# The last matrix product of a transformer block, cut into seven half-size products

## The chip, the core and the metric

The kernel runs on one core of a Trainium2 chip. The number compared is the device time of one execution, in microseconds (us), from the start of the program to its end. The core has a matrix engine (TensorE, PE in the profile, with its weight loads as PEld), a vector engine (VectorE, DVE), a scalar engine (ScalarE, ACT), a general engine (GpSimd, POOL) and a sync engine (SP), which here only issues DMA transfers. Each works through a queue of its own, in order, and waits on semaphores that the others raise.

## The reference, cut to what matters

Two transformer blocks are computed for 512 tokens of width 1024, with float32 inputs and output. The change is in the last line of the second block, a gated feed-forward layer with 2816 hidden features:

```python
FFN_HIDDEN = -(-(8 * D_MODEL) // (3 * 256)) * 256          # 2816 = 22 * 128
h = rms_norm(x, norm_ffn[l])
x = x + (jax.nn.silu(h @ w_gate[l]) * (h @ w_up[l])) @ w_down[l]
return x
```

The down projection multiplies a [512 x 2816] matrix, called A here, by `w_down`, [2816 x 1024], called B, and adds the product to x, which is the output.

## The kernel before, in words

**Three terms.** Each operand is split in two, both written in the type fp32r: the high part is a copy of the operand, the low part is the operand minus its high part. A product is three matmuls into the same bank of PSUM: high by high, low by high, high by low.

**Chunks.** The weights come in chunks of 128 rows by 512 columns, and all chunks of the kernel are in one list, `CH`. A slot of 8 KB per partition holds up to four chunks and is filled by one DMA; three slots (0, 1 and 2) take turns in the feed-forward layer. SyncE issues the DMAs in the order of the list, each when the slot's former chunks are used up (`slot_free`). For each chunk ScalarE writes the high part to one of eight places in `CHH` (so at most eight chunks can be ahead of TensorE: chunk c waits until c-8 is done), and VectorE then subtracts and writes the low part over the raw chunk (`low`). Both do this in `split_chunks`, called with the chunk number that is to be reached; `ahead(c, 5)` is five chunks beyond the one that TensorE is planned to use.

**Gate and up.** For four features at a time (of 128 hidden features each; 22 in all, the last turn has two) `fg` computes h @ w_gate, ScalarE applies silu, and `fu` computes h @ w_up. At the end of each `fu` VectorE multiplies the two (`up_evac`), ScalarE makes the high part of the product in `AFH`, and VectorE its low part in `AFL`. That gives A, transposed: feature by token.

**Down.** `seg("wd0")` and `seg("wd1")` compute the left and the right 512 columns of the output. Each goes over 22 chunks; for each chunk over four row blocks of 128 tokens, with three matmuls each: 2 x 22 x 4 x 3 = 528 matmuls of 512 columns. At the end of each half VectorE adds four banks to x in memory (`out_x`), and SyncE stores the result. GpSimd has nothing to do in this stage. The order of the work is written out by hand; there is no scheduler.

## Time and profile before

| | |
|---|---|
| median of three runs | 1574.17 us (1571.76 to 1575.76) |
| span of the profiled execution | 1570.6 us, from the first to the last instruction |
| TensorE busy | 1536.9 us, 98% |
| VectorE, ScalarE, GpSimd busy | 64%, 53%, 13% |
| first matmul of the down projection | begins at 1447.51 us |
| last matmul of the down projection | begins at 1566.96 us |

The profiled execution is one run of the same program; its span leaves out what lies before the first and behind the last instruction, so it is some 3.6 us below the median. TensorE's matmuls are pipelined: a row's duration (0.39 us) is longer than the step from one matmul to the next (0.23 us), and the step is what counts for time. For the other engines, instructions that are issued back to back also overlap a little, so that a group of several is shorter than its count times the duration of one.

### The profile page before, as it was taken

To read this page: it belongs to the slowest core of one execution; us is meant where nothing else is said; L and a number is where in the kernel's file an instruction comes from. 1 tells how busy PE (TensorE), PEld (TensorE's weight loads), DVE (VectorE), ACT (ScalarE), POOL (GpSimd) and SP (SyncE) were. 2 spreads that over 40 slices of the span, in tenths; PEclk is the share of its full clock that TensorE was granted. 3 is DMA by queue.
4 is the path that set the end of the run, shared out by engine and by line. 5 is a ranking of instruction groups with operands and counts; after the bars stand their busy time and mean duration, and the time that the engine had idled before them with its cause. 6 is when DMAs were issued, how large, how long until landed. Compare 5 with 4: busy or idle time off the path is not lost.

```text
span 1570.6 us, 20022 instructions
## 1 busy us (share of the span) xinstructions
PE 1536.9 (98%) x7872; PEld 1247.3 (79%) x7872; DVE 1007.2 (64%) x1681; ACT 832.5 (53%) x1459; POOL 210.5 (13%) x278
## 2 busy tenths in 40 slices
PE   9999999999999999999989999999999999999999
PEld 8877777788877888888877766888778888888887
DVE  4267977865479998999787786575765333434231
ACT  5278776554456888888863434435434333333220
POOL 1000014522234000000062101111201000000000
PEclk9999999999999999999999999999999999999999
DMA  6122121114547999999943111031212323223232
GB/s 233 65 81 79 56 71 65 54 54 150 214 161 231 375 421 421 421 422 421 326 149 107 54 54 54 28 108 54 81 58 78 108 81 108 92 82 121 67 112 90
DMA packets 78641, 235.89 MB, mean 150 GB/s; under 512 B 6960, under 2 KB 9424, under 8 KB 66256
## 3 DMA queue, kind: packets, MB, share of 16 engines
q1 hardware_dynamic: 68288, 207.62, 36.3%
q10 hardware_dynamic: 6624, 14.88, 2.5%
q0 software_dynamic: 3632, 12.08, 2.0%
q8 instruction: 63, 1.03, 0.3%
q14 instruction: 34, 0.28, 0.1%
HBM read 221.97 MB, written 12.60 MB: 149 GB/s over the span
## 4 chain that ended last, share of the span: by engine, by line
PE 84%; DVE 11%; ACT 2%; issue 1%; DMA 1%; POOL 0%; SPq 0%; DVEq 0%; ACTq 0%; POOLq 0%
PE bank L109 80%; PE bank L112 4%; DVE low L134 2%; DVE REST L124 1%; DVE REST L134 1%; DVE REST L137 1%; ACT REST L115 1%; DVE AL L124 1%; DVE REST L146 1%; DVE REST L143 1%; DVE REST L130 1%; ACT REST L118 1%; ACT CHH L118 0%; DVE R L124 0%; DVE st L140 0%
## 5 line engine op out<-in xcount | busy, mean ns | idle before, releaser
L124 DVE TENSOR_TENSOR low<-slot,CHH 128x1024 fp32r<-128x1024 f32 (+1 forms) x300 | 298.0, 1037 | 117.5 <-ACT CHH L118 116.5
L118 ACT ACTIVATE CHH<-slot 128x1024 fp32r<-128x1024 f32 (+1 forms) x300 | 258.8, 900 | 128.7 <-PE bank L109 56.6
L134 DVE SCALAR_TENSOR_TENSOR low<-slot,smalls,CHH 128x512 fp32r<-128x512 f32 (+1 forms) x232 | 170.3, 766 | 191.2 <-ACT CHH L118 187.3
L109 PE MATMUL bank<-AH,CHH 128*128 128x512 f32 (+1 forms) x640 | 248.5, 388 | 0.2 <-DVE AL L124 0.2
L109 PE MATMUL bank<-AL,CHH 128*128 128x512 f32 (+1 forms) x640 | 242.8, 379 | 0.0
L109 PE MATMUL bank<-AH,low 128*128 128x512 f32 (+1 forms) x640 | 242.6, 379 | 0.0
L118 ACT ACTIVATE CHH<-slot,smalls 128x512 fp32r<-128x512 f32 (+1 forms) x232 | 154.6, 701 | 137.8 <-PE bank L109 68.2
L109 PE MATMUL bank<-CHH,AH 128*128 128x512 f32 x512 | 215.2, 420 | 3.8 <-DVE low L134 2.8
L109 PE MATMUL bank<-low,AH 128*128 128x512 f32 x512 | 200.8, 392 | 0.0
L109 PE MATMUL bank<-CHH,AL 128*128 128x512 f32 x512 | 200.2, 391 | 0.0
L109 PE MATMUL bank<-CHH,XTF 128*128 128x512 f32 x512 | 161.2, 396 | 1.9 <-DVE REST L121 1.1
L109 PEld LDWEIGHTS bank<-AH,CHH 128*128 128x128 f32 x640 | 120.4, 188 | 23.3 <-issue 1.2
L109 PEld LDWEIGHTS bank<-AL,CHH 128*128 128x128 f32 x640 | 120.4, 188 | 23.1
L109 PEld LDWEIGHTS bank<-AH,low 128*128 128x128 f32 x640 | 120.6, 188 | 20.6
L115 ACT ACTIVATE REST<-REST 128x512 f32<-128x512 f32 (+4 forms) x193 | 98.0, 518 | 46.1 <-POOL REST L124 19.2
L109 PEld LDWEIGHTS bank<-CHH,AH 128*128 128x128 f32 x512 | 96.9, 189 | 29.6 <-issue 6.9
L109 PEld LDWEIGHTS bank<-low,AH 128*128 128x128 f32 x512 | 96.1, 188 | 21.3
L109 PEld LDWEIGHTS bank<-CHH,XTF 128*128 128x128 f32 x512 | 93.6, 188 | 24.0 <-DVE low L124 4.9
L109 PEld LDWEIGHTS bank<-CHH,AL 128*128 128x128 f32 x512 | 96.7, 189 | 14.9
L109 PE MATMUL bank<-low,XTF 128*128 128x512 f32 x256 | 99.9, 390 | 0.0
L118 ACT ACTIVATE REST<-bank 128x512 f32<-128x512 f32 (+6 forms) x166 | 62.5, 400 | 70.3 <-PE bank L112 40.7
L109 PE MATMUL bank<-REST 128*128 128x128 f32 (+8 forms) x688 | 90.0, 306 | 4.9 <-ACT REST L115 2.7
(191 smaller groups left out, 2395.4 us busy)
## 6 DMA issues: line engine op xcount, KB each, us to landing
slot<-in_w_in SPq DMA_DIRECT2D x35, 1024.0 KB, 5.1
slot<-in_w_exp_gate SPq DMA_DIRECT2D x32, 1024.0 KB, 13.0
slot<-in_w_exp_up SPq DMA_DIRECT2D x32, 1024.0 KB, 13.2
slot<-in_w_exp_down SPq DMA_DIRECT2D x32, 1024.0 KB, 13.2
slot<-in_w_gate SPq DMA_DIRECT2D x10, 1024.0 KB, 4.9
slot<-in_w_up SPq DMA_DIRECT2D x10, 1024.0 KB, 5.0
slot<-in_w_down SPq DMA_DIRECT2D x10, 1024.0 KB, 5.1
slot<-in_w_out SPq DMA_DIRECT2D x8, 1024.0 KB, 5.1
```

What stands on the lines that cost most here:

```text
L109: return self.e.matmul(out, l, r, start=start, stop=stop) if self.e else Issued()
L112: return self.e.transpose(out, in_, ident) if self.e else Issued()
L115: return self.e.activation(out, in_, f, scale=scale, bias=bias, accum_out=accum) if self.e else Issued()
L118: return self.e.activation(out, in_, ACT.Copy, scale=scale) if self.e else Issued()
L124: return self.e.tensor_tensor(out, a, b, op) if self.e else Issued()
L130: return self.e.tensor_scalar(out, a, s1, None, op0)
L134: return self.e.scalar_tensor_tensor(out=out, in0=a, scalar=s, in1=b, op0=op0, op1=op1) if self.e else Issued()
L137: return self.e.tensor_tensor_scan(out, a, b, initial, op0, op1) if self.e else Issued()
L143: return self.e.reciprocal(out, a) if self.e else Issued()
L146: return self.e.copy_predicated(out, mask, a) if self.e else Issued()
```

## The change

The down projection is done by a scheme with seven products instead of eight. A is cut into four quarters: A11 and A12 are the first 256 tokens with the first and last 11 features of 128, A21 and A22 are the other 256 tokens. B is cut into B11, B12, B21 and B22 in the same way (11 x 128 rows, 512 columns). The kernel forms

- S1 = A21 + A22, S2 = S1 - A11, S3 = A11 - A21, S4 = A12 - S2
- T1 = B12 - B11, T3 = B22 - B12, T2 = T3 + B11, T4 = B21 - T2 (with the sign as in the code)

and the products P1 = A11 B11, P2 = A12 B21, P6 = S2 T2 (on top of P1 in the same two banks), P7 = S3 T3, P4 = A22 T4, P3 = S4 B22, and P5 = S1 T1 (on top of P1 + P6). P6, P7 and P4 are taken chunk by chunk in turn, eleven times; P3 is the sixth and P5 the seventh. Each product has 11 chunks with two row blocks of three matmuls, so each chunk now serves 6 matmuls instead of 12. Products are added to the places of x that they belong to (`add_on`), 18 additions of 128 x 512.

New for each engine: GpSimd forms the sums of A (44 operations of 128 x 256) as VectorE delivers the features, makes the low parts of S3 and S2 in one instruction each (128 x 2816), and forms T2 and T4 (22 operations of 128 x 512) and T1 (11). VectorE forms T3 (11 of 128 x 512), splits 77 chunks instead of 44, and makes the low parts of A11 by feature (`first_low`) and of A12, A22, S1 and S4 whole (`low_of`, 128 x 2816). ScalarE makes the high parts of the same pieces (`high_of`). Each of the eleven middle slots ("quarters" in the code) holds one row of chunks of all of B11, B12, B21, B22; five slots take turns (9, 10, 1, 2, 0). P3's chunks and P1's and P2's are loaded plainly; B11 and B12 are loaded once more for T1.

On VectorE, where the down projection begins, before (`low` a low part of a chunk; `AFL` a low part of A; `R1` holds the gates):

```order
L124 TENSOR_TENSOR low1_85<-slot1_76,CHH_49 128x512 [waits act_hi] x4
L124 TENSOR_TENSOR low2_86<-slot2_77,CHH_49 128x512 [waits act_hi]
L124 TENSOR_TENSOR R1_50<-R1_50,bank0 128x512 [waits act_evac,pe_dense]
L124 TENSOR_TENSOR AFL_65<-R1_50,AFH_64 128x512 [waits act_evac]
L124 TENSOR_TENSOR R1_50<-R1_50,bank1 128x512 [waits slot_free]
L124 TENSOR_TENSOR AFL_65<-R1_50,AFH_64 128x512 [waits act_evac]
L124 TENSOR_TENSOR low2_86<-slot2_77,CHH_49 128x512 [waits act_hi] x3
L124 TENSOR_TENSOR low0_84<-slot0_75,CHH_49 128x512 [waits act_hi] x4
```

and now (`AR` raw pieces of A and its sums, `AO` their low parts, `HA0` to `HA4` high parts):

```order
L129 TENSOR_TENSOR low1_92<-slot1_81,CHH_49 128x512 [waits act_hi] x4
L129 TENSOR_TENSOR low2_93<-slot2_82,CHH_49 128x512 [waits act_hi]
L129 TENSOR_TENSOR AR_64<-R1_50,bank0 128x2x256 [waits act_evac,pe_dense]
L129 TENSOR_TENSOR AO_65<-AR_64,HA0_66 128x256 [waits pool_down]
L129 TENSOR_TENSOR AR_64<-R1_50,bank1 128x2x256 [waits act_evac,slot_free]
L129 TENSOR_TENSOR AO_65<-AR_64,HA0_66 128x256 [waits pool_down]
L129 TENSOR_TENSOR low2_93<-slot2_82,CHH_49 128x512 [waits act_hi]
L129 TENSOR_TENSOR AO_65<-AR_64,HA0_66 128x256 [waits pool_down]
L129 TENSOR_TENSOR low2_93<-slot2_82,CHH_49 128x512 [waits act_hi]
L129 TENSOR_TENSOR AO_65<-AR_64,HA2_68 128x2816 [waits pool_down,act_evac]
L129 TENSOR_TENSOR low2_93<-slot2_82,CHH_49 128x512 [waits act_hi]
L129 TENSOR_TENSOR low0_91<-slot0_80,CHH_49 128x512 [waits act_hi] x3
```

Chunk 5's and chunk 6's low parts stand between short low parts of A11, and the long low part of A12 stands ahead of chunk 7's.

GpSimd ended before ahead of this stage. Now its queue holds, from the last sums of A on:

```order
L129 TENSOR_TENSOR AR_64<-AR_64 128x256 [waits dve_evac]
L129 TENSOR_TENSOR AR_64<-AR_64 128x256 [waits pool_down] x2
L129 TENSOR_TENSOR AO_65<-AR_64,HA3_69 128x2816 [waits pool_down,act_evac]
L129 TENSOR_TENSOR AO_65<-AR_64,HA1_67 128x2816 [waits act_evac]
L129 TENSOR_TENSOR slot9_89<-slot9_89 128x512 [waits dve_down]
L129 TENSOR_TENSOR slot9_89<-slot9_89 128x512 [waits pool_down]
L129 TENSOR_TENSOR slot10_90<-slot10_90 128x512 [waits dve_down]
```

The two long subtractions (low parts of S3, then of S2) stand ahead of T2 and T4 of the first quarter, and T4 waits for T2.

On VectorE, in the third and fourth quarter (rows with `slotN<-slotN` are T3, `R2` is x):

```order
L129 TENSOR_TENSOR low10_101<-slot10_90,CHH_49 128x512 [waits act_hi]
L129 TENSOR_TENSOR slot1_81<-slot1_81 128x512 [waits w_land1]
L129 TENSOR_TENSOR low10_101<-slot10_90,CHH_49 128x512 [waits act_hi] x2
L129 TENSOR_TENSOR low1_92<-slot1_81,CHH_49 128x512 [waits act_hi]
L129 TENSOR_TENSOR R2_51<-bank4,R2_51 128x512 [waits dve_evac,pe_dense]
L129 TENSOR_TENSOR R2_51<-bank5,R2_51 128x512 [waits dve_evac,slot_free]
L129 TENSOR_TENSOR slot2_82<-slot2_82 128x512 [waits w_land2]
L129 TENSOR_TENSOR low1_92<-slot1_81,CHH_49 128x512 [waits act_hi] x2
L129 TENSOR_TENSOR low2_93<-slot2_82,CHH_49 128x512 [waits act_hi]
L129 TENSOR_TENSOR slot0_80<-slot0_80 128x512 [waits w_land0]
```

Where nothing is put between them, three low parts of chunks come after each T3; T2 of a quarter can start on GpSimd when its T3 is done, and the next T3 stands behind the low part of that T2.

The core of the diff:

```diff
-    for n in range(2):
-        plan_seg(f"wd{n}", t["w_down_2"][0], 512 * n, 0, nk=FT, part=3)
+    formed, formed_raw, formed_low = {}, {}, {}
+    down_rows = t["w_down_2"][0].rearrange("(t k p) n -> p t k n", t=2, p=P)
+    D0 = len(CH)
+    def plan_block(t_, n0):
+        for k in range(0, FK, 4):
+            m = min(4, FK - k)
+            s = plan_slot(next(in_turn), down_rows[:, t_, k:k + m, n0:n0 + 512], m, 512, 3)
+            CH.extend((s, q) for q in range(m))
+    plan_block(0, 0)
+    plan_block(1, 0)
+    down_turns = itertools.cycle((9, 10, next(in_turn), next(in_turn), next(in_turn)))
+    quarters = []
+    for j in range(FK):
+        s = plan_slot(next(down_turns), down_rows[:, :, j, :], 2, 1024, 3)
+        b11, b12, b21, b22 = quarter = [(h, slice(512 * n, 512 * n + 512)) for h in range(2) for n in range(2)]
+        quarters.append((s, len(CH)))
+        for name, q, raw_at, low_at in (("T2", 0, b11, b12), ("T3", 0, b22, b22), ("T4", 1, b21, b21)):
+            c = len(CH)
+            formed[c] = (name, j)
+            formed_raw[c] = s.ap[:, raw_at[0], raw_at[1]]
+            formed_low[c] = s.low[:, low_at[0], low_at[1]]
+            CH.append((s, q))
+    in_turn = down_turns
+    plan_block(1, 512)
+    for k in range(0, FK, 2):
+        m = min(2, FK - k)
+        s = plan_slot(next(down_turns), down_rows[:, 0, k:k + m, :], m, 1024, 3)
+        for q in range(m):
+            c = len(CH)
+            formed[c] = ("T1", k + q)
+            formed_raw[c], formed_low[c] = s.ap[:, q, 512:1024], s.low[:, q, 512:1024]
+            CH.append((s, q))
...
-        for n in range(2):
-            drain(seg(f"wd{n}", aT, lambda k, j: ("aT", k)))
+        def product(name, c, part, k, two, first, last):
+            hi, lo = high(c), low(c)
+            pe.wait_ge(*at(("part", part, k) if part == A11 else ("part", part)))
+            pe.wait_ge(*at(("", "lo", c)))
+            for i in range(2):
+                l = [x[:, k, i * P:(i + 1) * P] for x in (part_high[part], parts_low[:, part])]
+                pe.matmul_on(two[i], l[0], hi, first, False)
+                pe.matmul_on(two[i], l[1], hi, False, False)
+                m = pe.matmul_on(two[i], l[0], lo, False, last)
+                ev = [("full", name, i)] if last else []
+                if i == 1:
+                    ev.append(("", "done", c))
+                if ev:
+                    m.then_inc(*mark("slot_free" if i == 1 and ends_slot(c) else "pe_dense", *ev))
+        def pair(name):
+            two = [banks.use("main", (name, i)) for i in range(2)]
+            for _, old in two:
+                pe.wait_ge(*at(old))
+            return [b for b, _ in two]
+        sums = pair("P1")
+        for k in range(FK):
+            product("P1", D0 + k, A11, k, sums, k == 0, k == FK - 1)
+        own2 = pair("P2")
+        for k in range(FK):
+            product("P2", D0 + FK + k, A12, k, own2, k == 0, k == FK - 1)
+        own7, own4 = pair("P7"), pair("P4")
+        for i in range(2):
+            pe.wait_ge(*at(("on x", "P1", i, 0)))
+        for k in range(FK):
+            c = D0 + 2 * FK + 3 * k
+            product("P6", c, S2, k, sums, False, k == FK - 1)
+            product("P7", c + 1, S3, k, own7, k == 0, k == FK - 1)
+            product("P4", c + 2, A22, k, own4, k == 0, k == FK - 1)
+        banks.next["main"] += 2
+        own3 = pair("P3")
+        for k in range(FK):
+            product("P3", D0 + 5 * FK + k, S4, k, own3, k == 0, k == FK - 1)
+        for i in range(2):
+            pe.wait_ge(*at(("on x", "P6", 2 + i, 0)))
+        for k in range(FK):
+            product("P5", D0 + 6 * FK + k, S1, k, sums, False, k == FK - 1)
         banks.groups["main"] = (0, 1, 2, 3)
...
-                act.wait_ge(*landed(c))
+                act.wait_ge(*(at(formed[c]) if c in formed else landed(c)))
...
+        def high_of(part, *events):
+            for event in events:
+                act.wait_ge(*at(event))
+            act.copy(part_high[part], parts[:, part]).then_inc(*mark("act_evac", ("part high", part)))
+        gates_done = ("full", "fu20", 1)
+        beside = {0: lambda: high_of(A12, gates_done, ("a", FT - 1)), 2: lambda: high_of(S3, gates_done, ("S3", FK - 1)),
+                  5: lambda: high_of(S2, ("a", FT - 1), ("S2", FK - 1)), FK + 1: lambda: high_of(A22, ("", "done", D0 + FK - 1)),
+                  2 * FK + 2: lambda: high_of(S1, ("", "done", D0 + 2 * FK - 1)), 2 * FK + 6: lambda: high_of(S4, ("S4", FK - 1))}
+        for n in range(7 * FK):
+            split_chunks(ahead(D0 + n, 5))
+            if n in beside:
+                beside[n]()
...
+        def first_low(k):
+            dve.wait_ge(*at(("S2", k)))
+            dve.wait_ge(*at(("part high", A11, k)))
+            dve.tt(parts_low[:, A11, k, :], parts[:, A11, k, :], part_high[A11][:, k, :].bitcast(F32), ALU.subtract).then_inc(
+                *mark("dve_evac", ("part", A11, k)))
         for f0 in range(0, FT, 4):
             def up_evac(j, f0=f0):
                 f = f0 + j
-                s = sgp.buf(("sg", f))
+                of = A11 if f < FK else A12
                 dve.wait_ge(*at(("full", f"fu{f0}", j)))
                 dve.wait_ge(*at(("fgs", f)))
-                dve.tt(s, s, banks.ap((f"fu{f0}", j)), ALU.mult).then_inc(
-                    *mark("dve_evac", ("fum", f), ("free", (f"fu{f0}", j))))
-                dve.wait_ge(*at(("aTh", f)))
-                dve.tt(aT[1][:, f, :], s, aT[0][:, f, :].bitcast(F32), ALU.subtract).then_inc(
-                    *mark("dve_evac", ("aT", f), ("free", ("sg", f))))
+                dve.tt(parts[:, of:of + 2, f % FK, :], *(x.rearrange("p (t n) -> p t n", t=2) for x in (
+                    sgp.buf(("sg", f)), banks.ap((f"fu{f0}", j)))), ALU.mult).then_inc(
+                    *mark("dve_evac", ("a", f), ("free", (f"fu{f0}", j)), ("free", ("sg", f))))
+                if f > FK:
+                    first_low(f - FK - 1)
...
+        def low_of(part):
+            dve.wait_ge(*at(("part high", part)))
+            dve.wait_ge(*at(("S4", FK - 1)))
+            dve.tt(parts_low[:, part], parts[:, part], part_high[part].bitcast(F32), ALU.subtract).then_inc(
+                *mark("dve_evac", ("part", part)))
+        def third(k):
+            s, _ = quarters[k]
+            dve.wait_ge(sem(f"w_land{s.i}"), s.landed)
+            dve.tt(s.ap[:, 1, 512:1024], s.ap[:, 1, 512:1024], s.ap[:, 0, 512:1024], ALU.subtract).then_inc(
+                *mark("dve_down", ("T3", k)))
+        last_on = {(i, n): ("x4", i, n) for i in range(NT) for n in range(2)}
+        def add_on(name, half, n, bank=None, left=False, done=False):
+            for i in range(2):
+                to = 2 * half + i, n
+                xs = xr[:, to[0], n * 512:(n + 1) * 512]
+                dve.wait_ge(*at(("full", name, i)))
+                dve.wait_ge(*at(last_on[to]))
+                last_on[to] = ("on x", name, *to)
+                events = [last_on[to]]
+                if left:
+                    events.append(("free", (name, i)))
+                if done:
+                    events.append(("out", *to))
+                dve.tt(xs, banks.ap((bank or name, i)), xs, ALU.add).then_inc(*mark("dve_evac", *events))
+        beside = {0: lambda: first_low(FK - 1), 1: lambda: low_of(A12), FK + 1: lambda: add_on("P1", 0, 0),
+                  FK + 3: lambda: low_of(A22), 2 * FK + 1: lambda: add_on("P2", 0, 0, left=True, done=True), 2 * FK + 5: lambda: low_of(S1), 2 * FK + 10: lambda: low_of(S4)}
+        for k in range(FK):
+            beside[2 * FK + 3 * k - 8] = lambda k=k, other=beside.get(2 * FK + 3 * k - 8): (other and other(), third(k))
+        end = 5 * FK
+        for n in range(7 * FK):
+            split_chunks(ahead(D0 + n, 5))
+            if n in beside:
+                beside[n]()
+            if n == end - 1:
+                add_on("P6", 1, 0, bank="P1")
+            if n == end + 1:
+                add_on("P7", 1, 0)
+                add_on("P7", 1, 1)
+                add_on("P4", 1, 0, done=True)
+            if n == 6 * FK + 1:
+                add_on("P3", 0, 1)
+        add_on("P5", 1, 1, bank="P1", done=True)
+        add_on("P5", 0, 1, bank="P1", done=True)
...
+        for f in range(FT):
+            k = f % FK
+            pool.wait_ge(*at(("a", f)))
+            if f < FK:
+                pool.tt(parts[:, S3, k, :], parts[:, A11, k, :], parts[:, A21, k, :], ALU.subtract).then_inc(*mark("pool_down", ("S3", k)))
+            else:
+                pool.tt(parts[:, S1, k, :], parts[:, A21, k, :], parts[:, A22, k, :], ALU.add).then_inc(*mark("pool_down", ("S1", k)))
+                pool.wait_ge(*at(("S1", k)))
+                pool.tt(parts[:, S2, k, :], parts[:, S1, k, :], parts[:, A11, k, :], ALU.subtract).then_inc(*mark("pool_down", ("S2", k)))
+                pool.wait_ge(*at(("S2", k)))
+                pool.tt(parts[:, S4, k, :], parts[:, A12, k, :], parts[:, S2, k, :], ALU.subtract).then_inc(*mark("pool_down", ("S4", k)))
+        for part in (S3, S2):
+            pool.wait_ge(*at(("part high", part)))
+            pool.wait_ge(*at(("S4", FK - 1)))
+            pool.tt(parts_low[:, part], parts[:, part], part_high[part].bitcast(F32), ALU.subtract).then_inc(*mark("pool_down", ("part", part)))
+        for k in range(FK):
+            s, c = quarters[k]
+            b11, b21, t3 = s.ap[:, 0, 0:512], s.ap[:, 1, 0:512], s.ap[:, 1, 512:1024]
+            pool.wait_ge(*at(("T3", k)))
+            pool.tt(b11, t3, b11, ALU.add).then_inc(*mark("pool_down", ("T2", k)))
+            pool.wait_ge(*at(("T2", k)))
+            pool.tt(b21, b21, b11, ALU.subtract).then_inc(*mark("pool_down", ("T4", k)))
+        for k in range(FK):
+            s, q = CH[D0 + 6 * FK + k]
+            b11, b12 = s.ap[:, q, 0:512], s.ap[:, q, 512:1024]
+            pool.wait_ge(sem(f"w_land{s.i}"), s.landed)
+            pool.tt(b12, b12, b11, ALU.subtract).then_inc(*mark("pool_down", ("T1", k)))
...
+            elif s.i == 9 and s.former is None:
+                sp.wait_ge(*at(("full", "fu20", 1)))
+            elif s.i == 10 and s.former is None:
+                sp.wait_ge(*at(("", "done", D0 + FK - 1)))
```

## Rows read from the trace of the kernel before

**Rows 1.** the page: the span, the engines, TensorE's granted clock in 40 slices

```profile
span 1570.6 us, 20022 instructions
...
PE 1536.9 (98%) x7872; PEld 1247.3 (79%) x7872; DVE 1007.2 (64%) x1681; ACT 832.5 (53%) x1459; POOL 210.5 (13%) x278
...
PEclk9999999999999999999999999999999999999999
```

**Rows 2.** the chain that ended last, 1400 to 1571 us: start, length, what

```profile
1399.84 167.52 PE bank L109 x739
...
1567.38 0.69 DVE R L124
```

**Rows 3.** timeline, first and last matmul of the down projection (start, length, what)

```profile
1447.51 0.39 PE L109 MATMUL bank<-CHH,AFH 128*128 128x512 f32 x1
...
1566.96 0.39 PE L109 MATMUL bank<-low,AFH 128*128 128x512 f32 x1
```

**Rows 4.** groups by form, 1448 to 1571 us: count, busy us, mean ns, idle before

```profile
L124 DVE TENSOR_TENSOR low<-slot,CHH 128x512 fp32r<-128x512 f32 x40 | 26.4, 690 | 69.3 <-ACT CHH L118 69.3
L118 ACT ACTIVATE CHH<-slot 128x512 fp32r<-128x512 f32 x39 | 23.0, 626 | 71.5 <-DMA slot<-in_w_down 46.5 <-PE bank L109 25.0
```

**Rows 5.** timeline, ScalarE and VectorE where the down projection begins

```profile
1447.27 0.63 ACT L118 ACTIVATE CHH<-slot 128x512 fp32r<-128x512 f32 x1 [3.15 <-DMA slot<-in_w_down]
...
1447.94 0.69 DVE L124 TENSOR_TENSOR low<-slot,CHH 128x512 fp32r<-128x512 f32 x1 [2.85 <-ACT CHH L118]
1448.55 0.68 DVE L124 TENSOR_TENSOR R<-R,bank 128x512 f32<-128x512 f32 x1
...
1452.53 3.09 DVE L124 TENSOR_TENSOR low<-slot,CHH 128x512 fp32r<-128x512 f32 x5
```

**Rows 6.** GpSimd's sums: one group of the whole run, then timeline rows

```profile
L124 POOL TENSOR_TENSOR REST<-REST 128x256 f32<-128x256 f32 x52 | 40.4, 783 | 43.4 <-DVE R L124 41.5
...
249.31 1.30 POOL L124 TENSOR_TENSOR REST<-REST 128x256 f32<-128x256 f32 x2 [0.36 <-DVE R L124]
...
378.80 2.54 POOL L124 TENSOR_TENSOR R<-R,R 128x512 f32<-128x512 f32 x2 [32.41 <-DVE R L124]
...
1125.19 2.39 POOL L124 TENSOR_TENSOR VM<-REST,VM 128x1024 fp32r<-128x1024 f32 x1
```

**Rows 7.** groups of the whole run: the two forms of 1024 columns

```profile
L124 DVE TENSOR_TENSOR low<-slot,CHH 128x1024 fp32r<-128x1024 f32 x192 | 223.8, 1220 | 24.8 <-ACT CHH L118 23.8 <-issue 0.2
...
L118 ACT ACTIVATE CHH<-slot 128x1024 fp32r<-128x1024 f32 x192 | 195.2, 1057 | 31.4 <-PE bank L109 24.0 <-ACT R L118 6.1 <-DMA slot<-in_w_exp_down 1.2
```

**Rows 8.** timeline, three places where GpSimd and VectorE meet

```profile
457.33 3.85 POOL L124 TENSOR_TENSOR R<-REST 128x1024 f32<-128x1024 f32 x1 [1.16 <-ACT REST L118]
...
458.21 3.00 DVE L124 TENSOR_TENSOR REST<-REST 128x16 f32<-128x16 f32 x1
...
461.66 0.17 DVE L124 TENSOR_TENSOR REST<-REST 128x16 f32<-128x16 f32 x1
...
383.00 1.74 POOL L124 TENSOR_TENSOR R<-R,R 128x512 f32<-128x512 f32 x1
...
382.42 1.16 DVE L124 TENSOR_TENSOR low<-slot,CHH 128x512 fp32r<-128x512 f32 x1
...
383.51 1.78 DVE L124 TENSOR_TENSOR AL<-R,AH 128x512 fp32r<-128x512 f32 x1
...
377.97 2.05 DVE L124 TENSOR_TENSOR R<-bank,R 128x512 f32<-128x512 f32 x3 [3.68 <-PE bank L109]
```

**Rows 9.** DMA issues: KB each, median us to landing

```profile
slot<-in_w_down SPq DMA_DIRECT2D x10, 1024.0 KB, 5.1
```

**Rows 10.** windows at the end: TensorE busy (count), then the granted clock PEclk

```profile
1569.00:1569.50 0.50, 0.00 (x0) 0.00 (x0) 0.00 (x0) 0.00 (x0) 0.00 (x0) 0.82 1.02 393
1569.50:1570.00 0.50, 0.00 (x0) 0.00 (x0) 0.00 (x0) 0.00 (x0) 0.00 (x0) 0.50 0.32 119
```

**Rows 11.** timeline, VectorE's last additions

```profile
1565.35 2.73 DVE L124 TENSOR_TENSOR R<-bank,R 128x512 f32<-128x512 f32 x4 [18.36 <-PE bank L109]
```

More of the change, by code:

```diff
@@ L25 @@
 FT = 22
+FK = 11
+FH = 256
 EPS = 1e-6
@@ L109, in matmul, with matmul_on @@
         return self.e.matmul(out, l, r, start=start, stop=stop) if self.e else Issued()
+    def matmul_on(self, out, l, r, start, stop):
+        return self.e.matmul(out, l, r, start=start, stop=stop, skip_group_check=True) if self.e else Issued()
     def transpose(self, out, in_, ident):
```

40 lines of the change are left out of this document (19 added, 21 removed).

## The prediction, written before the changed kernel was run

> **What bounds the kernel now.** I read the page first, then the chain of waits, then the timeline of the last 120 us, then every row in which GpSimd adds. The page has TensorE busy for 98% of a span of 1570.6 us, at full clock in all slices [rows 1]. The chain that ended last is one unbroken run of matmuls from 1399.84 us to 1567.36 us, and behind it one addition [rows 2]. So in this stage a matmul less is a step less, if nothing else becomes late. The first of the 528 matmuls of the down projection starts at 1447.51 us and the last at 1566.96 us [rows 3]: 119.45 / 527 = 0.2267 us a step, 119.7 us in all. VectorE makes a low part in 0.69 us, or in 0.60 us where several follow each other ((3.09 - 0.69) / 4), and waits most of the time for ScalarE, which needs 0.63 us for a high part and waits for DMA and TensorE [rows 4, 5]. There is room on both. GpSimd is idle.
>
> The execution's own time is 1570.6 us of span; the median of the runs is 1574.2 us, 3.6 us more. I work in the span and add 3.6 us at the end. About 0.3% (5 us) is what a measurement can tell here.
>
> **What the change removes.** 7 products x 11 chunks x 6 matmuls = 462 instead of 528. 66 steps less are 66 x 0.2267 = 15.0 us, the whole possible gain. A chunk now lasts 6 x 0.2267 = 1.36 us on TensorE instead of 2.72 us, a product 15.0 us, a quarter (three chunks) 4.08 us.
>
> **The prices of what is added.** I count from T = 0, where the down projection starts.
> - VectorE, 128 x 512: 0.60 us, as above. 128 x 2816 is in no row. The step from 512 to 1024 columns is 1.220 - 0.690 = 0.53 us [rows 4, 7]; carried on, 2816 columns take 3.07 us. Bounds: 1.22 us (the nearest row) and 5.5 times 0.69, 3.8 us. I take 3.07, since all rows of this kind lie on one line.
> - ScalarE, 2816 columns, likewise: 0.626 + 4.5 x 0.431 = 2.6 us [rows 4, 7]; bounds 1.06 and 3.4 us.
> - GpSimd: 256 columns 0.65 us (1.30 for two), 512 columns 1.25 us (2.54 for two), 1024 columns 2.39 us [rows 6]. So 2816 columns take 2.39 + 3.5 x 1.14 = 6.4 us; bounds 2.39 us and 5.5 times 1.27, 7.0 us. The GPSIMD Engine Reference of the Trainium skill (Elementwise, side-by-side cycle accounting) has 4497 ns for 2048 columns with two inputs, by which one would estimate 6.2 us; two such instructions would shorten my sum by 0.4 us.
>
> **The two engines keep each other out.** This is the row that decides. At 458.21 us VectorE adds 16 columns, from memory to memory, and takes 3.00 us; the same form takes 0.17 us a little later. GpSimd's addition of 457.33 us ended at 461.18 us, just when VectorE got through [rows 8]. At 382.42 us a low part takes 1.16 us and the next 1.78 us, while GpSimd's own addition of 512 columns takes 1.74 us instead of 1.27: they go in turn, one whole instruction each. Additions that take one input from a bank (377.97 us, three in 2.05 us) run beside GpSimd at their usual speed, though GpSimd starts at 378.80 us [rows 6, 8]. Low parts and T3 have both inputs in memory, so they are of the kind that waits; `add_on` isn't.
>
> The page SBUF — State Buffer of the Trainium skill (SBUF: two separate sides) says the same as a rule: a VectorE instruction with two SBUF inputs and a GpSimd instruction that reads SBUF use one shared port pair, which is locked for the whole instruction. By that rule the new stage is slower, by its absence 13.8 us faster; the trace agrees with it in all three places.
>
> **The first product, step by step.** TensorE starts with chunks 0 to 4 ready: chunk 4's low part comes at 1447.94 us, T = 0.4, as now [rows 5]. VectorE then has two multiplications, the low parts of A11's last three features (each behind a sum S2 on GpSimd) and chunks 5 and 6. GpSimd needs six sums after feature 20 is there at about 1.5, each 0.65 us and in turn with VectorE: the last ends at 7.0. Chunk 6 is through at 7.6 (TensorE wants it at 8.2). Then VectorE makes the low part of A12 whole: 7.6 + 3.07 = 10.7. ScalarE has finished S3's high part by then (A12's from 2.5, S3's from about 6.1, 2.6 us each: 8.7), so GpSimd's long subtraction for S3 is waiting and gets its turn: 10.7 to 17.1. Chunk 7's low part stands behind it and comes at 17.7; TensorE wanted it at 7 x 1.36 = 9.5. It stands still for 8.2 us. Then GpSimd's second long one, for S2, has its turn: 17.7 to 24.1. Chunk 8 comes at 24.7, and TensorE, done with chunk 7 at 19.1, stands still for another 5.6 us. P1 ends at 24.7 + 3 x 1.36 = 28.8 instead of 15.0: 13.8 us lost.
>
> **To the first T3.** A22's high part overwrites A11's, so ScalarE starts it when P1 is done: 28.8 to 31.4. The third slot of P2 is freed at the same time and lands 5.1 us later [rows 9], 33.9; ScalarE and VectorE have chunk 19 at 35.1, then VectorE makes the low part of A22, 38.2, and T3 of the first quarter, 38.8. Quarters 0 and 1 are issued behind that slot; both are there for this. TensorE meanwhile does P2, 28.8 to 43.8, without a wait.
>
> **The quarters.** In each, VectorE has three low parts and T3, GpSimd T2 and T4, in a circle: T3, low part, T2, low part, T4, low part (it is that of T2, and the next T3 stands behind it). All six want the same turn: 4 x 0.60 + 2 x 1.25 = 4.9 us, against TensorE's 4.08. Bounds: 4.08 (hidden) and 4 x 0.69 + 2 x 1.74 = 6.2 us. Eleven are 53.9 us, less the 0.6 of a T3 that isn't there at the end. Two additions of P2, made while GpSimd waits for T3, add 1.2 us; the low parts of S1 and S4, which nothing needs yet, add 2 x 3.07 = 6.1 us. So chunk 52's low part comes at 38.8 + 53.3 + 1.2 + 6.1 = 99.4, and TensorE does chunks 52 to 54 until 103.5.
>
> **The rest.** P3 and P5 are 22 chunks, 29.9 us: the three engines have 22 low parts, 11 T1 and 10 additions for it (13.2 + 13.8 us in turn, the additions beside GpSimd), and the slots are freed early enough. The stage ends at 133.4 instead of 119.7: +13.7 us. Behind the last matmul come four additions instead of one: they start with the last but one bank, 0.7 us before the end, and take 4 x 0.6 us, so the end is later by 2.4 - 0.7 - 0.6 = 1.1 us [rows 11].
>
> **The clock.** After its last matmul TensorE keeps its full clock until about 1569.3 us and is at 1.2 GHz from 1569.5 us on, 2 us after 1567.4 [rows 3, 10]. Both waits in P1 are longer than that. At 1.2 GHz a chunk costs 1.36 us more; how long it takes to come back no row shows. Chunk 7 has room for it, chunks 8 to 10 don't: 0 to 4.1 us. I take one chunk, 1.4 us.
>
> Sum: 13.7 + 1.1 + 1.4 = +16.2, so 1586.8 us of span and about **1590 us** in the median.
>
> **At nothing.** The sums of A in the gate stage: 38 of 0.65 us, twelve at a time after `fu12` and `fu16`; VectorE's work between is hardly longer than the AFL and multiplication pairs that go, and TensorE has more than five chunks in hand. Were that not enough, a chunk late costs about 1 us in two places. DMA: a slot of 1 MB per 4.9 us, landing in 5.1 us, five slots. The wait of P6 for P1's two additions: they are done 10 us before.
>
> **Rivals.**
> 1. *The two engines do not meet*, since these operations are not of the kind in rows 8. Then TensorE sets the pace: -15.0 + 1.1 = -13.9, 1560 us. Against it: the low parts there are the same instruction as here. 13%.
> 2. *Only the front is late.* If GpSimd's T2 and T4 find their turn beside TensorE's 4.08 us (bare costs smaller than mine by 17%, or T3 further ahead), P1 costs 13.8 us and the rest is hidden: -15.0 + 13.8 + 1.1 + 1.4 = +1.3, 1575 us. For it: the sum of 4.9 is near 4.08. Against it: the circle has no slack, and the low parts of S1 and S4 fall into it. 13%.
> 3. *The clock stays low.* With a gap in every quarter and two long waits ahead, TensorE stays at 1.2 GHz through P2 (11 x 1.36 = 15 us more, of which the wait for T3 hides none of the delay to the first T3, but some of P2's). It decides if the clock isn't back within P1: +15 to 20 us above my sum without the clock term, 1605 us. 11%.
> The forecast has 63%, its own range 1581 to 1601 us: the circle by -0.4 and +0.6 us each, GpSimd's long two by 0.6 us each, the clock by 1.4 down and 2.7 up.
>
> The range for 8 in 10 is 1570 to 1602 us: rival 1 is left out, and most of rival 3. Faster by over 0.3%: 14% (rival 1 and a little). Within: 12% (rival 2's middle). Slower: 74%.
>
> **What would show it.** In the changed profile: TensorE idle for about 8 and 6 us in the first 25 us of the stage, each ending with a low part of a chunk that took over 6 us on VectorE; GpSimd's two instructions of 2816 columns at 6 to 7 us; VectorE's low parts at 1 to 2 us in the quarters, where GpSimd's of 512 columns take about 1.8; chunk groups in the quarters at 4.9 us. P3 and P5 without idle time. If the low parts stay at 0.69 us beside GpSimd, the forecast is wrong at its root; if the quarters take 4.1 us, at its second term.

## The result: 0.8% slower, and the profile after

The changed kernel took 1586.4 us in the median of four runs (1585.17 to 1589.09), the kernel before 1574.97 us beside it (1571.76 to 1576.49): a ratio of 1.008, with a 95% interval of 1.0064 to 1.0097. Forecast were 1590 us, within 1570 to 1602. In the profiled executions the span went from 1570.6 us [rows 1] to 1583.5 us, 12.9 us more. The stage begins at different times in different executions, by some microseconds that have nothing to do with it. So I count again from T = 0, where its first chunk begins: 1446.9 us in this trace.

The page of the changed kernel, its span and its engines. TensorE is busy 4.4 us less than in [rows 1], in 66 matmuls less; the span is longer all the same. GpSimd has 79 instructions more.

```profile
span 1583.5 us, 20133 instructions
...
PE 1532.5 (97%) x7806; PEld 1237.6 (78%) x7806; DVE 1087.8 (69%) x1728; ACT 858.7 (54%) x1487; POOL 318.9 (20%) x357
```

The chain that ended last in the changed kernel: start, length, what. In [rows 2] this stage was one run of matmuls. Now it goes through VectorE, GpSimd, ScalarE and a DMA until 1539.87 us, and TensorE sets the pace only after that.

```profile
1454.92 3.08 DVE AO L129
1458.00 13.12 DVE low L129 x2
1471.25 6.47 PE bank L114 x18
1477.74 4.51 DMA slot<-in_w_down
1482.28 0.64 ACT CHH L123
1482.94 0.69 DVE low L129
1483.63 3.00 DVE AO L129
1486.63 0.61 DVE slot L129
1487.32 1.69 POOL slot L129
1489.02 0.64 ACT CHH L123
1489.69 1.56 DVE low L129
...
1544.47 34.31 PE bank L114 x150
1578.81 0.69 DVE R L129
```

Two low parts took 13.12 us. The next view says why. It is the timeline of GpSimd in the changed kernel: start, length, what and how many, and in brackets the idle time before.

```profile
1455.76 14.80 POOL L129 TENSOR_TENSOR AO<-AR,HA 128x2816 fp32r<-128x2816 f32 x2 [1.32 <-ACT HA L123]
...
1487.32 3.38 POOL L129 TENSOR_TENSOR slot<-slot 128x512 f32<-128x512 f32 x2 [16.76 <-DVE slot L129]
...
1491.93 3.38 POOL L129 TENSOR_TENSOR slot<-slot 128x512 f32<-128x512 f32 x2 [1.23 <-DVE slot L129]
...
1540.49 3.38 POOL L129 TENSOR_TENSOR slot<-slot 128x512 f32<-128x512 f32 x2 [1.23 <-DVE slot L129]
```

GpSimd's two instructions of 2816 columns end at 1470.56 us. A12's low part on VectorE ran until about 1458.0 us (1454.92 and 3.08). In the 12.6 us between, GpSimd did its two and VectorE one low part of 0.6 us: 6.0 us each for GpSimd. The low part of chunk 7 stood behind the first, that of chunk 8 behind the second. From one T2 to the next are 4.60 us (1487.32 to 1491.93), and a low part ahead of it takes 1.56 us.

The groups of the stage by form, 1447 to 1584 us: count, busy us, mean ns, idle before. The low part answers to the first row of [rows 4]: 1238 ns instead of 690. ScalarE's high part stays at 626 ns, and VectorE's additions that read a bank are at 678 ns (687 before).

```profile
L129 DVE TENSOR_TENSOR low<-slot,CHH 128x512 fp32r<-128x512 f32 x73 | 87.6, 1238 | 11.5 <-ACT CHH L123 10.4
...
L123 ACT ACTIVATE CHH<-slot 128x512 fp32r<-128x512 f32 x73 | 43.1, 626 | 70.7 <-POOL slot L129 46.8 <-DMA slot<-in_w_down 15.7 <-PE bank L114 8.2
...
L129 DVE TENSOR_TENSOR R<-bank,R 128x512 f32<-128x512 f32 x18 | 11.3, 678 | 3.3 <-PE bank L114 3.3
```

TensorE's waits in the stage of the changed kernel, in all, how many, the longest; then the two in P1 in TensorE's timeline, with the wait in brackets; then windows, which print how long PE, PEld, DVE, ACT and POOL were busy (with the count) and then TensorE's granted clock.

```profile
PE bank L114 <- DVE low L129: 16.9, 5, 7.9
```

```profile
1464.71 0.77 PE L114 MATMUL bank<-CHH,HA 128*128 128x512 f32 x1 [7.93 <-DVE low L129]
...
1471.25 0.77 PE L114 MATMUL bank<-CHH,HA 128*128 128x512 f32 x1 [3.65 <-DVE low L129]
```

```profile
1456.00:1460.00 4.00, 0.77 (x4) 0.29 (x2) 4.00 (x2) 4.00 (x5) 4.00 (x1) 0.84 0.22 86
1460.00:1464.00 4.00, 0.00 (x0) 0.00 (x0) 4.00 (x1) 1.76 (x4) 4.00 (x2) 0.50 0.00 0
1464.00:1468.00 4.00, 2.90 (x6) 1.84 (x6) 4.00 (x2) 0.00 (x0) 4.00 (x2) 0.50 0.00 0
1468.00:1472.00 4.00, 0.75 (x2) 0.68 (x3) 4.00 (x3) 0.00 (x0) 2.56 (x1) 0.50 0.82 253
1472.00:1476.00 4.00, 4.00 (x12) 3.08 (x11) 3.92 (x7) 1.26 (x2) 0.00 (x0) 0.53 0.03 9
1476.00:1480.00 4.00, 4.00 (x19) 3.33 (x18) 1.89 (x3) 2.89 (x2) 0.00 (x0) 1.00 0.29 46
...
1512.00:1516.00 4.00, 2.73 (x7) 2.15 (x8) 4.00 (x5) 0.63 (x1) 2.17 (x2) 0.66 0.00 2
```

TensorE is at 1.2 GHz (0.50) from about 1458.7 us, within the first wait of P1, until about 1476 us. From 1471.25 us on it worked without a wait, and the 18 matmuls of chunks 8 to 10 took 6.47 us instead of the 4.08 us at 2.4 GHz. The clock falls once more at about 1513 us, in the wait of 3.9 us that ends behind the low part of S1.

### The profile page after: what moved, and what is told of

It reads as the page before. It is cut to its first block, busy times and chain, and to the rows that moved or that the text cites. A ratio compares the mean times of both kernels' runs of the same rounds, so it can differ in the third digit from the quotient of the medians.

```text
span 1583.5 us, 20133 instructions
## 1 busy us (share of the span) xinstructions
PE 1532.5 (97%) x7806; PEld 1237.6 (78%) x7806; DVE 1087.8 (69%) x1728; ACT 858.7 (54%) x1487; POOL 318.9 (20%) x357
## 3 DMA queue, kind: packets, MB, share of 16 engines
q1 hardware_dynamic: 71328, 222.04, 38.8%
## 4 chain that ended last, share of the span: by engine, by line
PE 77%; DVE 14%; ACT 3%; POOL 2%; DMA 2%; issue 1%; DVEq 0%; SPq 0%; POOLq 0%; ACTq 0%
PE bank L111 71%; PE bank L117 4%; PE bank L114 3%; DVE low L129 2%; DVE low L139 2%; DVE REST L139 1%; DVE REST L142 1%; DVE REST L129 1%; POOL slot L129 1%; ACT REST L120 1%; DVE AO L129 1%; ACT CHH L123 1%; DVE AL L129 1%; POOL AR L129 1%; DVE REST L151 1%
## 5 line engine op out<-in xcount | busy, mean ns | idle before, releaser
L129 DVE TENSOR_TENSOR low<-slot,CHH 128x1024 fp32r<-128x1024 f32 (+1 forms) x333 | 358.9, 1121 | 58.8 <-ACT CHH L123 56.8
L123 ACT ACTIVATE CHH<-slot 128x1024 fp32r<-128x1024 f32 (+1 forms) x333 | 278.3, 873 | 123.6 <-POOL slot L129 46.8
L139 DVE SCALAR_TENSOR_TENSOR low<-slot,smalls,CHH 128x512 fp32r<-128x512 f32 (+1 forms) x232 | 175.7, 787 | 202.6 <-ACT CHH L123 202.4
L111 PEld LDWEIGHTS bank<-AH,CHH 128*128 128x128 f32 x640 | 120.5, 188 | 24.0 <-issue 1.2
L111 PEld LDWEIGHTS bank<-CHH,AL 128*128 128x128 f32 x512 | 96.7, 189 | 14.8
L136 POOL TENSOR_SCALAR st<-st 128x1 f32<-128x1 f32 (+2 forms) x70 | 21.9, 313 | 426.9 <-ACT REST L120 276.1
```

Of the source, the lines that this page charges most:

```text
L111: return self.e.matmul(out, l, r, start=start, stop=stop) if self.e else Issued()
L123: return self.e.activation(out, in_, ACT.Copy, scale=scale) if self.e else Issued()
L129: return self.e.tensor_tensor(out, a, b, op) if self.e else Issued()
L136: return self.e.tensor_scalar(out, a, s1, s2, op0, op1)
L139: return self.e.scalar_tensor_tensor(out=out, in0=a, scalar=s, in1=b, op0=op0, op1=op1) if self.e else Issued()
```

## The experiments

All kernels were run beside the kernel before, which took 1574.5 us in the first group of four, 1574.6 us in the second four and 1575.1 us in the last. Ratios are to it. "Stage" is counted in the trace from T = 0 to the addition that begins the end of the chain (in the changed kernel 1446.87 to 1578.81 us), as the difference in spans also holds noise from ahead of the stage. It is read from one execution of each kernel. TensorE's waits are the idle times in its timeline; a wait costs about 0.3 us more than is printed, since the row before it is drawn 0.16 us longer than a step and the first step behind it is longer by 0.1 us.

| kernel | median us | ratio, 95% | stage us | TensorE's waits us (longest) |
|---|---|---|---|---|
| before | 1574.97 | 1 | 119.9 | none |
| changed | 1586.4 | 1.008 (1.0064 to 1.0097) | 131.9 | 16.9 (7.9) |
| e1: GpSimd's long two in pieces | 1582.7 | 1.0051 (1.0032 to 1.0070) | 127.1 | 13.2 (4.0) |
| e2: sums of B narrow | 1577.8 | 1.002 (1.001 to 1.003) | 120.5 | 11.6 (7.9) |
| e3: fills for the long two | 1577.7, one run | | 121.1 | 7.3 (4.0) |
| e4: GpSimd only makes S and T1 | 1570.9 | 0.9974 (0.9964 to 0.9983) | 114.2 | 4.7 (2.0) |
| f1: only the long two to VectorE | 1576.6 | 1.0019 (1.0009 to 1.0028) | 120.8 | 6.7 (2.6) |
| f3: only S1's low part later | 1588.1 | 1.0086 (1.0069 to 1.0103) | 130.9 | 16.1 (7.9) |
| f2: e4, spread out | 1569.2 | 0.9967 (0.9956 to 0.9979) | 113.2 | 5.5 (2.9) |
| f4: e4, only the front spread | 1569.8 | 0.9968 (0.9957 to 0.9979) | 113.3 | 5.3 (2.9) |
| g1: f4, two low parts later | 1569.9 | 0.9964 (0.9950 to 0.9978) | 113.2 | 5.1 (2.5) |

My theory was the prediction's: GpSimd's and VectorE's instructions keep each other out, one whole instruction at a time, and that costs 13 us at the front (two instructions of 2816 columns) and more again in the quarters (22 of 512 columns). The rivals: only the front counts; VectorE has too much work in any case; it isn't the meeting but the waiting behind GpSimd's results.

### e1: the long two in pieces

GpSimd makes the low parts of S3 and S2 feature by feature, 22 instructions of 256 columns.

```diff
-            pool.tt(parts_low[:, part], parts[:, part], part_high[part].bitcast(F32), ALU.subtract)...
+            for k in range(FK):
+                pool.tt(parts_low[:, part, k, :], parts[:, part, k, :], part_high[part][:, k, :].bitcast(F32), ALU.subtract)...
```

> The changed kernel, with GpSimd's two long subtractions (low parts of S3 and S2) issued as 11 pieces of 256 columns each. The work is the same. Theory A (each whole instruction holds the turn): chunk 7's low part waits for one piece of 0.65 us instead of 6.2 us, the two waits of TensorE in P1 shrink to about 3 us together, the clock is not lost there, the first T3 comes about 9 us earlier; 1577 us, against 1586 of the changed kernel. Rival B (it is the total of work on both engines that counts, or GpSimd's bandwidth, not the length of one instruction): no change, 1586 us.

Measured: 1582.7 us, 3.7 us faster than the changed kernel, between the two expectations. The timelines of GpSimd and VectorE in e1, in order of time:

```profile
1457.87 27.47 POOL L129 TENSOR_TENSOR AO<-AR,HA 128x256 fp32r<-128x256 f32 x22 [1.31 <-ACT HA L123]
...
1460.03 12.69 DVE L129 TENSOR_TENSOR low<-slot,CHH 128x512 fp32r<-128x512 f32 x11
...
1485.30 2.61 POOL L129 TENSOR_TENSOR slot<-slot 128x512 f32<-128x512 f32 x2
```

The low parts now pass between the pieces, 1.15 us each instead of one per 6 us, and the longest wait fell from 7.9 to 4.0 us. But 22 pieces take GpSimd 27.5 us in place of 14.8, since each gives VectorE a turn, and the first T2 stands behind them until 1485.30 us. So TensorE waits 2.5 us in P1 instead of 11.6 us, but 2.2 us at the end of P2 and 4.0 us at the first quarter, where it did not wait before; the first T2 comes at T = 36.4 instead of 40.4. The smaller size moved a good half of the front's wait and took away the rest.

### e2: the sums of B narrow

T2, T4 and T1 are formed in 64 of their 512 columns only; the rest of these sums is left out.

```diff
-            pool.tt(b11, t3, b11, ALU.add)...
+            pool.tt(b11[:, 0:64], t3[:, 0:64], b11[:, 0:64], ALU.add)...
```

> The changed kernel, but GpSimd forms T2, T4 and T1 in 64 of their 512 columns only; the other columns are left as they were loaded. Same instructions and waits, 0.2 us instead of 1.1 us each. Theory A: a quarter costs 4 x 0.6 + 2 x 0.25 = 2.9 us of turns, less than TensorE's 4.08, so from P2 on nothing waits; the front is as late as before. 1576 us. Rival C (the circle of T3, T2, ScalarE's high part and VectorE's low part is set by waits and by its order, not by the shared turn): quarters stay above 4.08 us and the time is above 1582 us.

Measured: 1577.8 us, 8.6 us less. One row of VectorE's front in e2, and GpSimd's first two sums of B:

```profile
1459.76 18.00 DVE L129 TENSOR_TENSOR low<-slot,CHH 128x512 fp32r<-128x512 f32 x10
...
1488.99 1.44 POOL L129 TENSOR_TENSOR slot<-slot 128x64 f32<-128x64 f32 x2 [16.59 <-DVE slot L129]
1491.77 1.43 POOL L129 TENSOR_TENSOR slot<-slot 128x64 f32<-128x64 f32 x2 [1.34 <-DVE slot L129]
```

The front is as late as in the changed kernel (18.00 us for the ten low parts that follow A12's, in both), and the circle of a quarter falls from 4.60 to 2.78 us, less than TensorE's 4.08: TensorE doesn't wait at all after P1. The handovers between the engines are as many as before. So it isn't they that cost; it is the time of GpSimd's instructions of 512 columns in the circle.

### e3: fills in place of the long two

The low parts of S3 and S2 are not computed but filled with zeros, by four instructions of GpSimd over 2816 columns that read nothing.

```diff
-            pool.tt(parts_low[:, part], parts[:, part], part_high[part].bitcast(F32), ALU.subtract)...
+            pool.memset(parts_low[:, part].bitcast(F32), 0.0)...
+            pool.wait_ge(*at(("set", part)))
+            pool.memset(parts_low[:, part].bitcast(F32), 0.0)...
```

> The changed kernel, but the low parts of S3 and S2 are filled with zeros by GpSimd (two fills of 128 x 2816 for each, about 2.6 us a fill) instead of being computed. Theory A1 (GpSimd keeps VectorE out only while it reads memory, as the page SBUF of the Trainium skill has it): chunk 7's low part takes 0.6 to 0.7 us beside the fills, P1 loses some 2 us. Theory A2 (any GpSimd instruction on memory keeps it out): chunk 7's low part takes about 3 us, one fill and its own time, and chunks 8 to 10 the same; P1 loses 8 us or more.

The one run took 1577.7 us, and TensorE's only wait in P1 is 2.0 us, as theory A1 had it. The reading rests on the timelines of GpSimd and VectorE in e3:

```profile
1458.93 9.85 POOL L154 MEMSET AO<- 128x2816 f32 x4 [1.30 <-ACT HA L123]
...
1461.10 4.89 DVE L129 TENSOR_TENSOR low<-slot,CHH 128x512 fp32r<-128x512 f32 x8
```

Eight low parts take 4.89 us beside 9.85 us of GpSimd's work: 0.61 us each, as when alone. So it isn't a busy GpSimd that stops VectorE. An instruction of GpSimd that reads memory does, one that only writes doesn't. SBUF — State Buffer of the Trainium skill (Who interferes with whom) says just that, that a VectorE instruction with two inputs in SBUF contends with a GpSimd instruction that reads SBUF and not with one that only writes it; this trace agrees.

### e4: the two engines kept apart

T2, T4 and the low parts of S3 and S2 go to VectorE; the low part of S1 is made in the sixth product instead of the fifth quarter. GpSimd keeps the sums of A and T1.

```diff
+            dve.wait_ge(*at(("T3", k)))
+            dve.tt(b11, t3, b11, ALU.add).then_inc(*mark("dve_down", ("T2", k)))
+            dve.wait_ge(*at(("T2", k)))
+            dve.tt(b21, b21, b11, ALU.subtract).then_inc(*mark("dve_down", ("T4", k)))
...
-        beside = {0: lambda: first_low(FK - 1), 1: lambda: low_of(A12), FK + 1: ...
+        beside = {0: lambda: first_low(FK - 1), 1: lambda: low_of(A12), 5: lambda: low_of(S3), 9: lambda: low_of(S2), FK + 1: ...
```

> The changed kernel with VectorE doing what GpSimd did in this stage but T1: T2 and T4 behind each T3, and the low parts of S3 and S2 (behind chunks 10 and 14); the low part of S1 is made in the sixth product. Theory A: VectorE has 0.6 us for what took 1.1 to 1.7 us of turns, its whole work in the 75 us of the first five products is some 72 us, so TensorE waits a few us in P1 and P2 and hardly later: 1564 us, faster than both. Rival D (VectorE, now nearly full, becomes the bound and the waits for its own results add up): 1574 us or more.

Measured: 1570.9 us, 1% faster than the changed kernel and 0.26% faster than the kernel before, though VectorE has 22 sums and two long low parts more. It is 7 us short of what I expected. VectorE's timeline in e4:

```profile
1483.20 1.89 DVE L129 TENSOR_TENSOR low<-slot,CHH 128x512 fp32r<-128x512 f32 x3
1485.01 2.13 DVE L129 TENSOR_TENSOR slot<-slot 128x512 f32<-128x512 f32 x3
1487.06 1.89 DVE L129 TENSOR_TENSOR low<-slot,CHH 128x512 fp32r<-128x512 f32 x3
1488.87 2.14 DVE L129 TENSOR_TENSOR slot<-slot 128x512 f32<-128x512 f32 x3
...
1505.50 3.08 DVE L129 TENSOR_TENSOR AO<-AR,HA 128x2816 fp32r<-128x2816 f32 x1
```

A quarter takes VectorE 3.86 us (1485.01 to 1488.87) of TensorE's 4.08, all from one engine, against 4.60 us where two engines share. It has 0.2 us to spare in a quarter, so the 3.0 us of S4's low part at 1505.50 us become a wait of 2.0 us. An equal wait stands in P1, and behind each of the two the clock fell:

```profile
1464.00:1468.00 4.00, 4.00 (x11) 3.12 (x12) 4.00 (x4) 2.95 (x5) 0.00 (x0) 0.61 0.11 20
...
1512.00:1516.00 4.00, 4.00 (x13) 3.10 (x12) 3.93 (x7) 1.67 (x3) 0.00 (x0) 0.58 0.04 16
```

With the small remainders in the next windows (0.97 and 0.99) that is 1.7 us of full-speed work lost each time, 3.4 us beside the 4.7 us of waits. The expectation had nothing for it.

### f1 and f3: one part at a time

f1 moves only the low parts of S3 and S2 to VectorE, and S1's to the sixth product (the second half of e4's diff). f3 moves only S1's.

```diff
-                  ... 2 * FK + 5: lambda: low_of(S1), 2 * FK + 10: lambda: low_of(S4)}
+                  ... 5 * FK + 3: lambda: low_of(S1), 2 * FK + 10: lambda: low_of(S4)}
```

> The changed kernel with the front alone mended: VectorE makes the low parts of S3 and S2 (behind chunks 10 and 14), that of S1 is made in the sixth product; T2, T4 and T1 stay on GpSimd. Theory A: the first T3 comes at about 29 us of the stage instead of 40, then ten quarters of 4.6 us, 1.2 us of additions and 3 us for S4: the stage is 13 to 14 us shorter than in the changed kernel, 1573 us. Rival (the front's delay is taken back in the quarters in any case, because these set the pace): under 5 us of gain, above 1581 us.

> The changed kernel, with one thing moved: the low part of S1 (VectorE, 3.07 us), which only the seventh product needs, is made in the sixth product instead of in the fifth quarter. Theory A: it lies in the circle, so 3.1 us go, and with them the wait behind which the clock fell at 1512 us, 1 us more: 1582 us. Rival (it fills time in which VectorE would have waited for GpSimd): no change, 1586 us.

These three make a ladder. f3 to f1, the long two: 1588.1 to 1576.6 us, 11.5 us (stage 10.2). f1 to e4, T2 and T4: 1576.6 to 1570.9 us, 5.7 us (stage 6.5). So the front is worth twice the quarters. Both missed my expectations. f1's rival is refuted, but f1 took 1576.6 us instead of 1573, and its stage is 11.2 us shorter than the changed kernel's instead of 13 to 14. f3's 1588.1 us is no faster than the changed kernel; its stage has only 1.0 us less, not 3.1. The chain in f3 shows where it came back:

```profile
1552.21 1.87 DVE R L129 x3
1554.08 1.20 DVE low L129 x2
1555.28 3.00 DVE AO L129
1558.28 1.69 DVE low L129
...
1560.02 1.67 PE bank L114 x6
```

In the sixth product VectorE makes six additions, S1's low part and the chunks' low parts in a row, and TensorE, which so far was behind VectorE, has caught up and waits there, 1.3 us in f3 and 1.5 us in f1.

### f2, f4 and g1: spreading VectorE's work

f4 is e4 with the last two features of A11, and the low parts of A12, S3 and S2, moved apart in P1 (after chunks 6, 7, 9, 12 and 15 have been split), and ScalarE's high parts of S3 and S2 one and two chunks later; f2 also makes S4's low part feature by feature just before P3. g1 is f4 with A22's low part moved behind the first quarter's sums, and S1's three chunks later.

```diff
-        beside = {0: lambda: first_low(FK - 1), 1: lambda: low_of(A12), 5: lambda: low_of(S3), 9: lambda: low_of(S2), ...
+        beside = {1: lambda: first_low(FK - 2), 2: lambda: first_low(FK - 1), 4: lambda: low_of(A12), 7: lambda: low_of(S3), 10: lambda: low_of(S2), ...
...
-                  FK + 3: lambda: low_of(A22), ... 5 * FK + 3: lambda: low_of(S1), ...
+                  17: lambda: low_of(A22), ... 61: lambda: low_of(S1), ...
```

> All of VectorE's work as in the kernel with its sums on VectorE, but spread: the low parts of A11's last two features behind chunks 6 and 7, those of A12, S3 and S2 behind chunks 9, 12 and 15, and that of S4 feature by feature where the sixth product begins, with TensorE waiting for it by feature. Theory A: TensorE has no wait above 1 us in P1 and none in the quarters (3.86 us each against 4.08): 1563 us. Rival D (VectorE is full, and what is moved comes back as a wait elsewhere): 1568 us or more.

> The same, but with the low part of S4 whole in the quarters (3.07 us) as in the changed kernel. Theory A: some 3 us of wait and 1 us of clock in the quarters come back: 1567 us. Rival D: the same time as the kernel that spreads S4 too.

> f4_front_spread with two low parts on VectorE moved: that of A22 from in front of the first T3 to behind the first quarter's T3, T2 and T4 (in f4 it stands at 1475.77 to 1478.86 us, and TensorE waits 2.91 us until 1481.57 us for the low part behind the sums), and that of S1 three chunks later, away from the six additions. Theory E (these waits are queueing at single places, VectorE has room elsewhere): the 2.9 us and about 1 us of the clock behind it go, 1566 us. Rival D (VectorE has no slack in the quarters, 3.9 us of work in 4.1): the 3.1 us of A22's low part turn up as a wait one or two quarters later, 1569 to 1570 us.

All three take 1569 to 1570 us, 0.3% less than the kernel before, and their stages have nearly the same length, 113.2 to 113.3 us. That is 0.9 us less than e4's, though TensorE's waits are longer (f4: 5.3 us, e4: 4.7). The clock makes the difference: in f4 it fell once in the stage (0.82 and 0.75 in the two windows from 1480 to 1488 us), which costs 1.7 us, in e4 twice. In f4 TensorE waits 2.9 us at 1478 to 1482 us, in front of the first quarter, behind A22's low part. In g1 that low part stands elsewhere, and the wait comes back behind it and the second quarter's sums, at chunk 23. The timelines of VectorE and TensorE in g1, and the window behind them:

```profile
1482.47 3.09 DVE L129 TENSOR_TENSOR AO<-AR,HA 128x2816 fp32r<-128x2816 f32 x1
1485.47 2.14 DVE L129 TENSOR_TENSOR slot<-slot 128x512 f32<-128x512 f32 x3
...
1488.27 0.61 PE L114 MATMUL bank<-CHH,HA 128*128 128x512 f32 x1 [2.49 <-DVE low L129]
```

```profile
1488.00:1492.00 4.00, 3.73 (x9) 2.94 (x10) 3.93 (x8) 1.81 (x5) 0.00 (x0) 0.57 0.17 69
```

Rival D was right in the times, and g1's trace shows for which stretch. VectorE shows no idle time from 1461.78 us (T = 9.9) to TensorE's last wait, which ends at 1511.77 us (T = 59.9) with the low part of chunk 38. Where the 3 us of A22's low part stand in it is then of no account. TensorE's 38 chunks by there need 51.7 us; 5.1 us are waits, and the rest the restarts behind them and the clock. The 39 chunks that are left take 53.4 us without a wait, and 59.9 + 53.4 is the stage. Behind chunk 38 VectorE gains on TensorE, 3.86 against 4.08 us a quarter: the low part of chunk 52 is done at T = 76.4, and TensorE begins it at about T = 79. So VectorE lacks room ahead of T = 60, not up to the end of the quarters.

f2 fits this: it has the 3.0 us of S4's low part out of the quarters. The wait of 0.96 us that f4 has there (until 1508.93 us) is gone, but one comes in the sixth product, behind S1's low part:

```profile
1540.36 0.50 PE L114 MATMUL bank<-CHH,HA 128*128 128x512 f32 x1 [1.14 <-DVE AO L129]
```

g1, with S1's low part three chunks later, has no wait there. The two moves were not run together, and nothing was put into the 3.3 us (2.60 and 0.70) in which g1's VectorE waits for ScalarE ahead of T = 9.9. That no order of this work does better is not shown.

## Why the prediction was right, and what was mis-sized

The direction, the mechanism and the places were right. Step by step, in T (1446.9 us is zero):

1. **The two engines keep each other out.** Shown: e3 takes away the reading and the low parts are at 0.61 us; e4 takes away the meeting and the stage is 16.7 us shorter than in f3. Rival 1 (13%) is refuted as the forecast of this kernel. Its 1560 us aren't reached by e4 either, where VectorE has to do what GpSimd leaves.
2. **GpSimd's long two.** I took 6.4 us each, within 2.39 to 7.0; it was 6.0. The figure of the GPSIMD Engine Reference of the Trainium skill (Elementwise, side-by-side cycle accounting), by which I estimated 6.2 us, was nearer than my line through 512 and 1024 columns. TensorE's waits in P1: forecast 8.2 and 5.6 us, measured 7.9 and 3.7. The second is shorter because chunk 7 ran at 1.2 GHz and so used time in which TensorE would have waited; this I had said of chunk 7, but not taken off the 5.6. TensorE began chunk 8 at T = 24.4 (forecast 24.7).
3. **The clock.** Forecast one chunk, 1.4 us, out of 0 to 4.1. Measured: chunks 8 to 10 took 6.47 instead of 4.08 us, 2.4 us. P1 ended at T = 30.9; forecast 28.8 and 1.4, 30.2. Rival 3 (11%) didn't happen: the clock was back to 2.4 GHz by 1476 us, well within P2. The second fall, at about 1513 us, I hadn't foreseen; the chain there runs over VectorE and GpSimd, so it costs nothing.
4. **To the first T3.** Forecast 38.8 and the clock's 1.4, 40.2. The first T2 starts at 1487.32 us, T = 40.4. That it agrees so closely is in part luck: P1 ended 0.7 us later than forecast, and the slot behind it landed in 4.5 us instead of 5.1.
5. **The quarters: the step that was mis-sized.** I took 4.9 us a circle, 4 x 0.60 + 2 x 1.25; it was 4.60. From the first T2 to the eleventh are 53.2 us (1487.32 to 1540.49) where I had 49 + 1.2 + 6.1 = 56.3. The additions and the two long low parts have cost what I said (53.2 - 46.0 = 7.2); the whole difference of 3.1 us is ten circles at 0.3. GpSimd's 512 columns take 1.10 us in this circle ((4.60 - 4 x 0.60) / 2), while the row from which I had 1.25 us was of instructions alone. I took a price with its start in it; where an instruction stands ready and waits for its turn, the start is behind it already. That reading of the 0.15 us is argued, not shown. Rival 2 (13%) needs 4.08 us and has not come true, though e2 shows what it would look like: 2.78 us, and no wait of TensorE after P1.
6. **P3 and P5.** Forecast 29.9 us without idle time. The chain has 150 matmuls in 34.31 us, 25 chunks at 1.37; the last 22 are 30.2 us. Right.
7. **The end.** Forecast 1.1 us more. From the addition at 1578.81 us to the end of the span are 4.7 us; before they were 3.2 (1567.38 to 1570.6, [rows 2]). That is 1.5 us more.

The sum: forecast 13.7 + 1.4 for the stage, it was 131.9 - 119.9 = 12.0 us; the end 1.5 instead of 1.1; and the stage began 0.6 us earlier. 12.0 + 1.5 - 0.6 = 12.9, the difference in span. Almost all of the 3 us that I forecast too much is the circle. The medians differ by 11.4 us; the 1.5 us to the difference in span is inside what single executions scatter (each kernel's runs span 4 to 5 us). For the median I had added 3.6 us to the span, as the kernel before had it; here it is 2.9 (1586.4 - 1583.5). Single executions have about 2.4 us between their time and their span before and 1.9 us now; the rest is scatter. The 1590 was 3.6 us too high, 3.3 of it in the span. The lower end of my own range, 1581 us, doesn't follow from the terms that I named for it: 11 x 0.4 + 2 x 0.6 + 1.4 = 7.0, so 1583 us.

"At nothing" I had the sums of A, the DMA and P6's wait. No wait of TensorE ahead of chunk 7 shows, as forecast. The 14.4 MB more of DMA traffic never end a wait of TensorE in P3 or P5.

f3 and e4 are where I was wrong, and for one reason. I priced a step that is moved at what it costs where it stood, and took the place where it went as free. In f3 the 3.1 us were to go; the chain of the sixth product took 2 of them back. In e4 I had taken VectorE's spare time as a sum over five products; the work is crowded ahead of T = 60, and the room is behind. And I had left out the clock, 3.4 of the 7 us.

## What to carry to other kernels

Count an engine's idle time stretch by stretch against the engine that sets the pace; a new piece of work fits only where its stretch has room, and moving it about within a full stretch changed the stage by 0.1 us here (f4, g1). Before giving VectorE's work to GpSimd, ask whether both read memory at the same time: here 22 sums of 512 columns and two of 2816 were faster on the busier engine than shared between the two. And a long instruction on an engine that excludes another is a wait as long as itself for whatever stands behind; cutting it in pieces helps the one who waits and delays its own result (in e1 GpSimd's two were done at T = 36.4 instead of 23.7).

A change that takes 15 us of matmuls away has returned, at its best here, 5 us (f2, f4, g1). Of the rest, what TensorE waits for (5.1 to 5.5 us) and the clock behind it (1.7 us in f4) are read; they come from VectorE's work in the first 60 us, but for f2's last wait.
